# Queries stacked in 4 KB rows, early scores, panels prepared first, and unread dense products in the attention of a hybrid encoder

## The chip, the cores and the metric

The kernel runs on one core of a Trainium2 chip. The metric is device time in microseconds, as the median of the timed runs. Matrix products run on TensorE (PE in the profile), the rest on VectorE (DVE), ScalarE (ACT) and GpSimd (POOL); SyncE (SP) and ScalarE issue transfers.

## The reference

Two layers over 512 tokens of width 1024: a gated DeltaNet mixer, then sliding-window attention, each followed by an MLP and a gated per-layer embedding. The change is in the attention of the second layer:

```python
proj = h @ w_in + b_in                        # 16 query heads, 4 key/value heads of 64
q = apply_rope(proj[..., :qd] ...)            # pairs (i, i + 32) of a head are rotated
k = apply_rope(proj[..., qd:qd + kd] ...)
scores = einsum("bnqhgd,bnkhd->bnhgqk", q, kb) * 64 ** -0.5   # chunks of 64, this and the one before
m = maximum(max(scores), sink)
probs = exp(scores - m) / (sum(exp(scores - m)) + exp(sink - m))
o = einsum("bnhgqk,bnkhd->bnqhgd", probs, vb)
mix = o @ w_out + b_out
```

All is float32. The kernel splits operands of the large products in a rounded upper part (fp32r) and a remainder, and adds three products.

## The kernel before, in words

Each engine has its program, and all order between them is by semaphores. `product` (L146) issues the three matmuls of one split product. A weight matrix comes as panels of 2048 columns of 128 rows, numbered through the kernel. For each panel SP loads `wRaw`, ScalarE rounds it (`prep_hi`, L124, copy at L132) and VectorE makes the remainder (`prep_lo`, L135, L140), all in two slots; a slot's load waits for the remainder of the panel two before.

The attention has six panels, `N_SW` to `N_SW + 5`: the keys, four query panels (head j of each of the four groups; every panel has a first and a second rotary half, f = 0 and 1), and the values. `att_pe` (L1739) makes for each of the first five panels two tiles of 128 x 512 in banks 0 and 1, of 8 x 3 matmuls each, and waits for `qk_t` before it writes a bank again. `att_dve` (L1894) first makes the remainder of the next panel, then scales both tiles out of the banks (L1909), applies the rotation (L1915 to L1921) to `rot`, and takes the lower parts (L1926) once ScalarE has rounded the upper ones (`qkHi`, L1847). The parts live in the memory of `aH` and `aL`; the keys and each query panel have two rows of 512.

The scores need the rows in another order, head dimensions on 64 partitions and positions along the row. `stack` (L1702) moves them by transfers from one place of the on-chip memory to another: for each half and part, 4 transfers of 64 KB with pieces of 256 bytes for queries, 8 of 32 KB for keys. SP moves the upper parts, between its loads (`att_sp`, L1718), ScalarE the lower ones, in between its copies (`att_act`, L1834). TensorE makes the value panel, then waits for all of them and for `v_ok`.

Then come 16 blocks (`ATB`), i = 4 t + g: 128 positions, one key/value head with its four query heads. `scores(i)` writes 12 matmuls into bank i mod 4, VectorE takes maxima (`maxima`), ScalarE exponentials (`exps`, L1860), VectorE the probabilities (L1970, L1972), TensorE transposes them (L1828), ScalarE or VectorE copies them (`keep` L1872, L1982), and `values` (L1812 to L1815) multiplies them with the values; `out_hi` and `out_lo` split the result. TensorE is two blocks ahead with its scores and one behind with its values. In block 4 (`i == KVH`) ScalarE and VectorE also prepare the first panel of the output projection (L1890, L1986). After block 15 comes `out_pe`, then the second MLP.

## Time and profile before

| | us |
|---|---|
| timed runs | 1500.47, 1511.27, 1516.33 (median 1511.27) |
| profiled execution, its own time | 1499.67 |
| its span | 1497.70 |
| TensorE busy | 1455.9 (97%) |
| VectorE busy | 801.1 (53%) |
| ScalarE busy | 541.9 (36%) |
| mean granted clock of TensorE | 0.979 |

Durations and places in the span are those of the profiled execution; its time is 1.97 us over its span. A matmul's busy time in the profile includes its modelled end, so the starts of two successive ones tell the pace. In the timeline a number in brackets is the idle time before an instruction, with what ended it.

### The profile page before, as it was taken

How to read it: one execution, taken by the hardware profiler on the slowest of the kernel's cores; microseconds unless marked ns; L12 is line 12 of the kernel's file. 1: busy time of each engine (PE TensorE's matmuls, PEld its weight loads, DVE VectorE, ACT ScalarE, POOL GpSimd, SP SyncE). 2: the span in 40 equal slices, each digit the busy share in tenths (PEclk: the TensorE clock that was granted, in tenths of full speed). 3: DMA queues.
4: the chain of work that ended last, by engine and by line, in shares of the span. 5: the costliest groups of instructions: out<-in, count | busy, mean ns of one | idle time of the engine just before them, and what ended most of it. 6: DMA issues, size and time to landing. Idle time of an engine off the chain costs nothing.

```text
span 1497.7 us, 19380 instructions
## 1 busy us (share of the span) xinstructions
PE 1455.9 (97%) x7270; PEld 1202.1 (80%) x7270; DVE 801.1 (53%) x1132; ACT 541.9 (36%) x820; POOL 268.0 (18%) x269
## 2 busy tenths in 40 slices
PE   7899999999989999999999999999999999999998
PEld 5788888888877888888888777866888888888877
DVE  5555666666647434334356587556443443434655
ACT  7334343434225314232243442244341322314344
POOL 5644444535203100000002120000200000000211
PEclk9999999999999999999999999769999999999998
DMA  6212121110112232323222328511323223232221
GB/s 174 60 29 57 29 57 40 44 49 21 43 56 92 92 112 85 112 84 103 94 85 86 111 57 169 113 29 43 113 85 112 85 92 105 84 112 85 85 85 56
DMA packets 163810, 120.73 MB, mean 81 GB/s; under 512 B 44417, under 2 KB 161442, under 8 KB 163746
## 3 DMA queue, kind: packets, MB, share of 16 engines
q1 hardware_dynamic: 152210, 116.71, 26.1%
q10 hardware_dynamic: 11536, 3.15, 1.0%
q8 instruction: 42, 0.69, 0.2%
q14 instruction: 22, 0.18, 0.0%
HBM read 112.50 MB, written 2.10 MB: 77 GB/s over the span
## 4 chain that ended last, share of the span: by engine, by line
PE 79%; DVE 10%; ACT 4%; issue 3%; DVEq 1%; DMA 1%; ACTq 1%; SPq 1%; POOL 0%; POOLq 0%
PE psum L148 22%; PE psum L150 22%; PE psum L149 21%; PE psum L830 3%; PE psum L821 3%; DVE wL L140 2%; ACT wH L132 1%; PE psum L837 1%; DVE bL L1274 1%; ACT taps L676 1%; DVE hT L1475 1%; PE psum L1828 1%; DVE acc L1473 1%; PE psum L784 1%; PE psum L785 0%
## 5 line engine op out<-in xcount | busy, mean ns | idle before, releaser
L148 PE MATMUL psum<-aH,wH 128*128 128x512 f32 x896 | 363.0, 405 | 5.2 <-DVE wL L140 3.2
L150 PE MATMUL psum<-aL,wH 128*128 128x512 f32 x896 | 350.6, 391 | 0.0
L149 PE MATMUL psum<-aH,wL 128*128 128x512 f32 x896 | 349.9, 391 | 0.0
L140 DVE TENSOR_TENSOR wL<-wRaw,wH 128x2048 fp32r<-128x2048 f32 (+2 forms) x126 | 250.7, 1993 | 135.5 <-ACT wH L132 129.9
L148 PE MATMUL psum<-bH,wH 128*128 128x512 f32 x720 | 285.0, 396 | 5.7 <-DVE pleT L1909 3.2
L150 PE MATMUL psum<-bL,wH 128*128 128x512 f32 x720 | 280.8, 390 | 0.0
L149 PE MATMUL psum<-bH,wL 128*128 128x512 f32 x720 | 280.6, 390 | 0.0
L132 ACT CAST wH<-wRaw 128x2048 fp32r<-128x2048 f32 (+2 forms) x110 | 199.2, 1815 | 192.0 <-PE psum L150 191.8
L148 PEld LDWEIGHTS psum<-aH,wH 128*128 128x128 f32 x896 | 169.2, 189 | 37.1 <-DVE wL L140 3.4
L150 PEld LDWEIGHTS psum<-aL,wH 128*128 128x128 f32 x896 | 168.6, 188 | 36.3
L149 PEld LDWEIGHTS psum<-aH,wL 128*128 128x128 f32 x896 | 169.2, 189 | 30.6 <-issue 0.5
L148 PEld LDWEIGHTS psum<-bH,wH 128*128 128x128 f32 x720 | 135.5, 188 | 35.2 <-DVE wL L140 4.3
L150 PEld LDWEIGHTS psum<-bL,wH 128*128 128x128 f32 x720 | 135.3, 188 | 28.6
L149 PEld LDWEIGHTS psum<-bH,wL 128*128 128x128 f32 x720 | 135.5, 188 | 27.2 <-issue 0.5
L1460 DVE TENSOR_TENSOR hid<-hid 128x512 f32<-128x512 f32 x64 | 44.3, 692 | 149.4 <-ACT hid L1443 149.4
L1284 POOL COPY sqSum<-sqT 128x512 f32<-128x512 f32 x6 | 3.9, 649 | 656.4 <-ACT sqT L1267 641.9
L1470 DVE TENSOR_TENSOR acc<-psum,acc 128x512 f32<-128x512 f32 x64 | 44.2, 690 | 137.3 <-PE psum L150 137.3
L1443 ACT ACTIVATE hid<-psum 128x512 f32<-128x512 f32 x64 | 38.4, 600 | 208.1 <-PE psum L150 208.0
L929 ACT COPY xScaled<-psum 128x512 f32<-128x512 f32 x56 | 33.0, 589 | 154.3 <-PE psum L837 126.5
L1287 POOL TENSOR_TENSOR sqSum<-sqSum,sqT 128x512 f32<-128x512 f32 x40 | 55.7, 1392 | 135.5 <-ACT sqT L1267 114.7
L676 ACT ACTIVATE taps<-psum,colsB 128x512 f32<-128x512 f32 (+1 forms) x96 | 58.1, 690 | 15.2 <-DVE work L703 11.3
L830 PEld LDWEIGHTS psum<-xScaled 128*128 128x128 f32 x384 | 46.5, 191 | 21.2 <-ACT xScaled L929 13.9
(291 smaller groups left out, 1730.8 us busy)
## 6 DMA issues: line engine op xcount, KB each, us to landing
wRaw<-in_mlp_w_up SPq DMA_DIRECT2D x64, 512.0 KB
wRaw<-in_mlp_w_down SPq DMA_DIRECT2D x64, 512.0 KB
wRaw<-in_dn_w_in SPq DMA_DIRECT2D x32, 512.0 KB
wRaw<-in_ple_w_gate SPq DMA_DIRECT2D x16, 512.0 KB
wRaw<-in_sw_w_in SPq DMA_DIRECT2D x16, 256.0 KB
wRaw<-in_sw_w_out SPq DMA_DIRECT2D x16, 256.0 KB
wRaw<-in_dn_w_out SPq DMA_DIRECT2D x8, 384.0 KB
work<-in_x SPq DMA_DIRECT2D x4, 512.0 KB, 4.9
```

What stands on the lines that cost most here:

```text
L132: last = [nc.scalar.copy(o, r) for o, r in zip(panel_parts(wH, slot, n, True), panel_parts(wRaw, slot, n, False))][-1]
L140: last = [nc.vector.tensor_tensor(o, r, h_.bitcast(F32), ALU.subtract) for o, r, h_ in zip(*([v if half is None else v[:, half * v.shape[1 ...
L148: nc.tensor.matmul(o, wh, xh, start=first, stop=False)
L149: nc.tensor.matmul(o, wl, xh, start=False, stop=False)
L150: return nc.tensor.matmul(o, wh, xl, start=False, stop=last)
L676: last = nc.scalar.activation(taps[:, c, c:S], bank[b % 2][:, 0:S - c], ACT.Copy, scale=convW[:, CONV - 1 - c, bass.ds(b * HEADS_A + h, 1)])
L821: per_tile(lambda t: nc.tensor.matmul(bank[BY][:, rng(t)], lowT[:, t, :], inv[:, t, :], start=True, stop=True)).then_inc(t_done, 1)
L830: per_tile(lambda t: nc.tensor.matmul(bank[BX][:, rng(t)], invT[:, t, :], tMask[:, t, :], start=True, stop=True)).then_inc(p_done, 1)
L1287: nc.gpsimd.tensor_tensor(sqSum[:], sqSum[:], sqT[:, m % 2, :], ALU.add).then_inc(sq_used, 1)
L1443: nc.scalar.activation(hid[:, m % 2, :], bank[m % 2], ACT.Relu).then_inc(hid_f, 1)
L1460: nc.vector.tensor_tensor(hid2[:, m % 2, :], hid[:, m % 2, :], hid[:, m % 2, :], ALU.mult)
L1470: nc.vector.tensor_tensor(acc[:, m, :], bank[4 + m % 2], acc[:, m, :], ALU.add).then_inc(down_read, 1)
```

## The change

The upper and lower parts of two successive query panels are now written interleaved by chunk, one row of 1024 for each half (`placed`, `by_chunk`), so one transfer moves 32 partitions of 4 KB into `qS`, 8 for two panels and one part. The keys are written sorted by even and odd chunk and move in 8 transfers of 64 KB instead of 16. `stack(queue, w, i)` moves the keys (w = 0), query panels 1 and 2 (w = 1), and 3 and 4 (w = 2). SP issues the keys' upper part after it has loaded panel `N_SW + 4`, and the query stacks after its last load; ScalarE issues the lower ones in iterations 2, 4 and at the end.

On ScalarE the rounding of a panel comes ahead of the rotated rows of the panel before; on VectorE the remainder of panel j + 2 comes right behind the evacuation of panel j, ahead of its rotation.

TensorE makes, once the keys and the first query stack are there, the first head pair's half of the scores of blocks 0 to 3; it waits for the values ahead of the third. Then it issues `keep_clock(10)`: ten 128x128 by 128x512 matmuls into bank 7, whose results nothing reads. It waits for the second stack, makes the other half of blocks 0 and 1, and issues 8 more; blocks 0 to 3 have 5 more each ahead of their wait for the probabilities, and blocks 0 and 1 of the loop make the other half of the scores of blocks 2 and 3.

```diff
--- before.py
+++ after.py
@@ -1647,7 +1647,19 @@
 
         mlp_mem.close()
 
-        qkHi, qkLo = [[a[:, 2 * i:2 * i + 2, :] for i in range(4)] for a in (aH, aL)]
+        def stack_parts(a):
+            rows = [a[:, 2 * i:2 * i + 2, :].rearrange("p a b -> p (a b)") for i in range(4)]
+            return [[rows[0][:, f * S:(f + 1) * S] for f in range(2)], rows[1:3], [rows[3], rows[0]]]
+        qkHi, qkLo = stack_parts(aH), stack_parts(aL)
+
+        def placed(parts, j, f):
+
+            if j == 0:
+                return parts[0][f].rearrange("p (o m c) -> p m o c", o=2, c=CH)
+            return parts[1 + (j - 1) // 2][f].rearrange("p (n r c) -> p n r c", r=2, c=CH)[:, :, (j - 1) % 2]
+
+        def by_chunk(rows, j):
+            return rows.rearrange("p (m o c) -> p m o c", o=2, c=CH) if j == 0 else rows.rearrange("p (n c) -> p n c", c=CH)
 
         qS = sb("qS", [P, 2, 2, 2, S // CH, 2, CH], F32R)
         kS = sb("kS", [P, 4 * S + 2 * P], F32R)
@@ -1663,10 +1675,9 @@
         qk_r = sem("qk_r")
         qk_hi = sem("qk_hi")
         qk_lo = sem("qk_lo")
-        hi_moved = [sem("hi_moved0"), sem("hi_moved1")]
-        lo_moved = [sem("lo_moved0"), sem("lo_moved1")]
-        k_hi_moved = [sem("k_hi_moved0"), sem("k_hi_moved1")]
-        k_lo_moved = [sem("k_lo_moved0"), sem("k_lo_moved1")]
+        hi_moved = [sem("k_hi_moved"), sem("qa_hi_moved"), sem("qb_hi_moved")]
+        lo_moved = [sem("k_lo_moved"), sem("qa_lo_moved"), sem("qb_lo_moved")]
+        MOVED = 16 * 2 * KVH
         v_ok = sem("v_ok")
         sc_done = sem("sc_done")
         sc_read = sem("sc_read")
@@ -1699,21 +1710,19 @@
                 for r in range(2):
                     sp.dma_start(dst[r * HD:(r + 1) * HD, a], src[a, r]).then_inc(panel_in[n % 2], PANEL_INC // 4)
 
-        def stack(queue, j, f, i):
-
-            ready, part, moved = ((qk_hi, qkHi, hi_moved if j else k_hi_moved), (qk_lo, qkLo, lo_moved if j else k_lo_moved))[i]
-            queue.wait_ge(ready, 2 * j + f + 1)
-            for g in range(KVH):
-                src = part[j % 4][g * HALF:(g + 1) * HALF, f, :].bitcast(F32)
-                r = (g // 2) * HD + f * HALF
-                if j:
-                    dst = qS[r:r + HALF, (j - 1) // 2, g % 2, i, :, (j - 1) % 2, :]
-                    queue.dma_start(dst.bitcast(F32), src.rearrange("p (n c) -> p n c", c=CH)).then_inc(moved[f], 16)
-                    continue
-                c0 = (2 * (g % 2) + i) * S
-                for odd in range(2):
-                    dst = kS[r:r + HALF, c0 + odd * S // 2:c0 + (odd + 1) * S // 2].rearrange("p (m c) -> p m c", c=CH)
-                    queue.dma_start(dst.bitcast(F32), src.rearrange("p (m o c) -> p m o c", o=2, c=CH)[:, :, odd]).then_inc(moved[f], 16)
+        def stack(queue, w, i):
+
+            ready, part, moved = ((qk_hi, qkHi, hi_moved), (qk_lo, qkLo, lo_moved))[i]
+            for f in range(2):
+                queue.wait_ge(ready, 4 * w + f + 1)
+                for g in range(KVH):
+                    src = part[w][f][g * HALF:(g + 1) * HALF].bitcast(F32)
+                    r = (g // 2) * HD + f * HALF
+                    if w:
+                        dst = qS[r:r + HALF, w - 1, g % 2, i].rearrange("p n r c -> p (n r c)")
+                    else:
+                        dst = kS[r:r + HALF, (2 * (g % 2) + i) * S:(2 * (g % 2) + i + 1) * S]
+                    queue.dma_start(dst.bitcast(F32), src).then_inc(moved[w], 16)
 
         def att_sp(sp):
 
@@ -1724,14 +1733,10 @@
                     load_rotary(sp, j - 1)
                 else:
                     load_square(sp, N_SW + j, square_panel(sw_w_in[0], 0, D + (256 if j else 0)))
-                if j in (2, 3):
-                    stack(sp, 0, j - 2, 0)
-                elif j >= 4:
-                    for f in range(2):
-                        stack(sp, j - 3, f, 0)
-            for j in range(3, GRP + 1):
-                for f in range(2):
-                    stack(sp, j, f, 0)
+                if j == GRP:
+                    stack(sp, 0, 0)
+            stack(sp, 1, 0)
+            stack(sp, 2, 0)
             for j in range(4):
                 sp.wait_ge(panel_lo, N_SWOUT + j - 1)
                 load_mixer_out(sp, j)
@@ -1776,14 +1781,7 @@
                 if t % 2:
                     last.then_inc(tile_done, 1)
 
-            for f in range(2):
-                pe.wait_ge(k_hi_moved[f], 16 * KVH * 2)
-                pe.wait_ge(k_lo_moved[f], 16 * KVH * 2)
-                pe.wait_ge(hi_moved[f], 16 * KVH * GRP)
-                pe.wait_ge(lo_moved[f], 16 * KVH * GRP)
-            pe.wait_ge(v_ok, NT)
-
-            def scores(i):
+            def scores(i, heads=range(2)):
                 t, g = i // KVH, i % KVH
                 if i >= 4:
                     pe.wait_ge(sc_read, i - 3)
@@ -1791,13 +1789,19 @@
                 for c in range(2):
                     apart = S // 2 if c else S // 2 - CH
                     nk = 2 if c or t else 1
-                    for jp in range(2):
+                    for jp in heads:
                         o = bank[i % 4][:, (2 * c + jp) * P:(2 * c + jp) * P + nk * CH].rearrange("p (a k) -> p a k", a=nk)
                         q = [qS[rows, jp, g % 2, part, 2 * t + c].rearrange("p r c -> p (r c)") for part in range(2)]
                         k = [kS[rows, (2 * (g % 2) + part) * S + t * CH:(2 * (g % 2) + part) * S + t * CH + 2 * apart]
                              .rearrange("p (a k) -> p a k", a=2)[:, 0:nk, 0:CH] for part in range(2)]
                         last = product(o, q[0], q[1], k[0], k[1], True, True)
-                last.then_inc(sc_done, 1)
+                if 1 in heads:
+                    last.then_inc(sc_done, 1)
+
+            def keep_clock(count):
+
+                for _ in range(count):
+                    nc.tensor.matmul(bank[7], wH[:, n % 2, 0:P], X[0][:, 0, :], start=True, stop=True)
 
             def values(i):
 
@@ -1814,12 +1818,26 @@
                     nc.tensor.matmul(o[:, 0:2 * P], vT[0:CH, 0, d], probsT[i % 2][0:CH, 0:2 * P], start=True, stop=True)
                 nc.tensor.matmul(o[:, 2 * P:4 * P], vT[:, t, d], probsT[i % 2][:, 2 * P:4 * P], start=True, stop=True).then_inc(pv_done, 1)
 
-            scores(0)
-            scores(1)
+            for w in range(2):
+                pe.wait_ge(hi_moved[w], MOVED)
+                pe.wait_ge(lo_moved[w], MOVED)
+            pe.wait_ge(qk_t, 2 * GRP + 2)
+            for i in range(4):
+                if i == 2:
+                    pe.wait_ge(v_ok, NT)
+                scores(i, [0])
+            keep_clock(10)
+            pe.wait_ge(hi_moved[2], MOVED)
+            pe.wait_ge(lo_moved[2], MOVED)
+            scores(0, [1])
+            scores(1, [1])
+            keep_clock(8)
             for i in range(ATB):
                 t = i // KVH
                 if i + 2 < ATB:
-                    scores(i + 2)
+                    scores(i + 2, [1] if i < 2 else range(2))
+                if i < KVH:
+                    keep_clock(5)
                 pe.wait_ge(pr_ok, i + 1)
                 if i >= 2:
                     pe.wait_ge(pt_ok[i % 2], i // 2)
@@ -1833,20 +1851,23 @@
 
         def att_act(act, u, O):
             n0 = N_SW
+
+            def upper(j):
+                for f in range(2):
+                    act.wait_ge(qk_r, 2 * j + f + 1)
+                    if j == 3 and f:
+                        act.wait_ge(hi_moved[0], MOVED)
+                    nc.scalar.copy(placed(qkHi, j, f), by_chunk(rot[2 * f], j)).then_inc(qk_hi, 1)
             for j in range(GRP + 1):
                 prep_hi(act, n0 + j + 1, (n0 + j + 1) % 2)
                 if j == 0:
                     norm_act(act, u - 1)
+                if j in (2, 4):
+                    stack(act, j // 2 - 1, 1)
                 if j:
-                    for f in range(2):
-                        stack(act, j - 1, f, 1)
-                for f in range(2):
-                    act.wait_ge(qk_r, 2 * j + f + 1)
-                    if j >= 4:
-                        act.wait_ge(k_hi_moved[f], 16 * KVH * 2)
-                    nc.scalar.copy(qkHi[j % 4][:, f, :], rot[2 * f]).then_inc(qk_hi, 1)
-            for f in range(2):
-                stack(act, GRP, f, 1)
+                    upper(j - 1)
+            upper(GRP)
+            stack(act, 2, 1)
             a_ = nc.scalar
 
             def exps(i):
@@ -1895,18 +1916,18 @@
             v = nc.vector
             n0 = N_SW
             tt, st = v.tensor_tensor, v.scalar_tensor_tensor
+            prep_lo(dve, n0 + 1, (n0 + 1) % 2)
+            norm_dve(dve, u - 1)
+            dve.wait_ge(n_ok, norms_bc(u - 1))
+            dve.wait_ge(rope_ok, 1)
             for j in range(GRP + 1):
-                prep_lo(dve, n0 + j + 1, (n0 + j + 1) % 2)
-                if j == 0:
-                    norm_dve(dve, u - 1)
                 dve.drain()
-                if j == 0:
-                    dve.wait_ge(n_ok, norms_bc(u - 1))
-                    dve.wait_ge(rope_ok, 1)
                 r0 = R_BQ + 2 * (j - 1) if j else R_BK
                 for f, tf in enumerate((t1, t2)):
                     dve.wait_ge(tile_done, tiles_before(n0 + j) + f + 1)
                     tt(tf, bank[f], rBC[:], ALU.mult).then_inc(qk_t, 1)
+                if j < GRP:
+                    prep_lo(dve, n0 + j + 2, (n0 + j + 2) % 2)
                 dve.drain()
                 b1, b2 = colsB[:, r0:r0 + 1], colsB[:, r0 + 1:r0 + 2]
                 if j:
@@ -1921,9 +1942,9 @@
                 tt(rot[2], rot[2], rot[3], ALU.add).then_inc(qk_r, 1)
                 for f in range(2):
                     dve.wait_ge(qk_hi, 2 * j + f + 1)
-                    if j >= 4:
-                        dve.wait_ge(k_lo_moved[f], 16 * KVH * 2)
-                    tt(qkLo[j % 4][:, f, :], rot[2 * f], qkHi[j % 4][:, f, :].bitcast(F32), ALU.subtract).then_inc(qk_lo, 1)
+                    if j == 3 and f:
+                        dve.wait_ge(lo_moved[0], MOVED)
+                    tt(placed(qkLo, j, f), by_chunk(rot[2 * f], j), placed(qkHi, j, f).bitcast(F32), ALU.subtract).then_inc(qk_lo, 1)
             for a in range(2):
                 rows = slice(a * CH, (a + 1) * CH)
                 for c in range(2):
```

## Rows read from the trace of the kernel before

**Rows 1.** Page, part 2: granted clock in 40 slices, tenths of full speed.
```profile
PEclk9999999999999999999999999769999999999998
```

**Rows 2.** Windows: us, busy us per engine (x instructions), granted clock, DMA share, GB/s.
```profile
942.00:953.90 11.90, 11.90 (x98) 11.65 (x96) 7.33 (x16) 1.22 (x2) 0.79 (x2) 1.00 0.51 106
953.90:957.00 3.10, 0.05 (x2) 0.05 (x1) 0.88 (x2) 0.00 (x0) 1.59 (x4) 0.99 0.96 214
957.00:1001.40 44.40, 42.83 (x160) 31.14 (x160) 22.31 (x76) 18.43 (x88) 0.00 (x0) 0.50 0.27 59
1001.40:1030.90 29.50, 25.86 (x161) 18.29 (x160) 21.24 (x62) 16.43 (x75) 0.00 (x0) 1.00 0.00 1
```

**Rows 3.** PE timeline, attention: start, us, line, names, [idle before <-releaser].
```profile
956.98 0.39 PE L148 MATMUL psum<-kS,qS 64*128 64x64 f32 x1 [3.05 <-DMA qS<-aL]
...
964.62 1.06 PE L1828 MATMUL psum<-ident,acc 128*64 128x128 f32 x4 [0.52 <-DVE acc L1970]
...
985.85 1.11 PE L1828 MATMUL psum<-ident,acc 128*128 128x128 f32 x4
...
992.85 1.12 PE L1828 MATMUL psum<-ident,acc 128*128 128x128 f32 x4 [1.05 <-DVE acc L1972]
...
998.55 1.11 PE L1828 MATMUL psum<-ident,acc 128*128 128x128 f32 x4
...
1001.59 0.27 PE L149 MATMUL psum<-kS,qS 64*128 64x128 f32 x1
1001.70 0.27 PE L150 MATMUL psum<-kS,qS 64*128 64x128 f32 x1
...
1002.91 0.66 PE L1828 MATMUL psum<-ident,acc 128*128 128x128 f32 x4
...
1009.67 0.66 PE L1828 MATMUL psum<-ident,acc 128*128 128x128 f32 x4
```

**Rows 4.** PE timeline, end of panel 2 and start of panel 3.
```profile
916.52 0.39 PE L148 MATMUL psum<-bH,wH 128*128 128x512 f32 x1
916.75 0.39 PE L149 MATMUL psum<-bH,wL 128*128 128x512 f32 x1
...
920.38 0.47 PE L148 MATMUL psum<-bH,wH 128*128 128x512 f32 x1 [1.66 <-DVE pleT L1909]
```

**Rows 5.** Groups of DVE by form, 896 to 954: busy, mean ns, idle before.
```profile
L140 DVE TENSOR_TENSOR wL<-wRaw,wH 128x1024 fp32r<-128x1024 f32 x6 | 7.1, 1222 | 3.9 <-ACT wH L132 3.9
L1909 DVE TENSOR_TENSOR pleT<-psum,rBC 128x512 f32<-128x512 f32 x10 | 6.7, 690 | 4.2 <-PE psum L150 2.0 <-ACT rBC L1317 1.8
...
L1915 DVE SCALAR_TENSOR_TENSOR pleT<-pleT,colsB,ropeC 128x512 f32<-128x512 f32 x5 | 3.8, 752 | 0.5
```

**Rows 6.** Tile qS, 946 to 958: issue ns min/median/max, first and last start; landing.
```profile
L1711 ACTq DMA_DIRECT2D qS<-aL x8: 592/638/822, 948.2 to 953.0; - x8
...
DMA to landing us min/median/max: 2.1/2.1/3.7
```

**Rows 7.** DMA view, 949 to 953 (stacking) and 4.5 to 7.5 (loads of x).
```profile
DMA packets 3029, 0.73 MB, mean 182 GB/s; under 512 B 3029, under 2 KB 3029, under 8 KB 3029
...
DMA packets 349, 1.25 MB, mean 418 GB/s; under 512 B 43, under 2 KB 43, under 8 KB 349
```

**Rows 8.** ACT timeline, block 4's preparation.
```profile
987.48 1.90 ACT L132 CAST wH<-wRaw 128x2048 fp32r<-128x2048 f32 x1
```

**Rows 9.** DVE timeline, block 4's preparation.
```profile
989.42 2.29 DVE L140 TENSOR_TENSOR wL<-wRaw,wH 128x2048 fp32r<-128x2048 f32 x1 [2.21 <-ACT wH L132]
```

**Rows 10.** PE timeline, another wait, in the DeltaNet loop.
```profile
441.77 0.80 PE L784 MATMUL psum<-vNew,trig 128*128 128x128 f32 x2 [2.94 <-DVE vNew L986]
```

**Rows 11.** Windows behind that wait, columns as in rows 2.
```profile
441.60:445.00 3.40, 3.23 (x12) 2.94 (x13) 0.70 (x3) 0.00 (x0) 0.00 (x0) 0.51 0.71 216
445.00:448.00 3.00, 3.00 (x19) 2.42 (x19) 1.25 (x4) 0.37 (x1) 0.00 (x0) 1.00 0.31 104
```

## The prediction

> **What bounds the kernel.** The page's slices first: TensorE is busy nearly everywhere, and in two slices of forty its granted clock falls to 0.7 and 0.6 of full speed [rows 1]. The windows by stage put that in one place. Up to 953.9 TensorE works at full clock on the dense projection of the values; it then idles about 3 us, and from 957.0 to 1001.4 the attention's blocks run at clock 0.50, the lower level (1.2 GHz). From 1001.4 to 1030.9 the same kind of block runs at 1.00 (2.4 GHz) [rows 2]. The timeline of PE gives the price: between the transposes of blocks 5 and 6 lie 5.70 us at half clock, between those of blocks 7 and 9 6.76 us at full clock, so 3.38 us a block [rows 3]. A full-size block at half clock costs **2.32 us** more. The change works on this stretch and on the projections ahead of it; after 1030.9 TensorE has the next dense product ready and everything shifts as one, so what the attention ends earlier, the kernel ends earlier.
>
> Basis: the profiled execution took 1499.67 us for a span of 1497.70. The three timed runs are 1500.47, 1511.27 (the median, 11.6 above the profiled one) and 1516.33.
>
> **Projections, panels first.** Before, TensorE waits 1.66 us at 920.38 in front of the third query panel [rows 4]. The chain behind it: SP issues eight key transfers ahead of the panel's load, ScalarE rounds it late, and VectorE's remainder comes last. After, no transfer stands between SP's loads up to the panel at `N_SW + 4`, and both preparing engines take the next panel ahead of the rotation. VectorE's work per panel is 2 evacuations (0.69 each), a remainder of 2 x 1.22 (started 0.1 us apart, so 2.35), 4 rotations (0.75 each in the row, started some 0.67 apart), 2 sums and 2 lower parts of 0.69 [rows 5]: some 9.2 us. TensorE's 48 products at 0.227 us [rows 4] take 10.9 us. By my count of the order, the first evacuation of the next panel ends 10.7 to 11.4 us after the last tile of the one before, just when TensorE needs the bank: a wait of up to 0.3 us remains. **Gain 1.6 us**; bounds 0 (the wait turns into one for the bank) and 1.66. The key transfers lie beside products. On SP the next load queued behind them waits for a remainder that comes later anyway, and ScalarE's eight issues of about 0.64 us [rows 6] end before the rotated rows it next waits for. The value projection thus ends at 952.3 instead of 953.9.
>
> **Stacking.** Transfers that must follow the last query panel grow from 16 of 64 KB to 16 of 128 KB, since panels 3 and 4 share a row: 2.1 MB. SP can issue from about 945.7, ScalarE from 946.4, eight each at about 0.63 us, and the median landing is 2.1, the longest 3.7 [rows 6]. At the rate of loads in 4 KB rows, 418 GB/s [rows 7], the issues bound it and the last lands at 953.9. At the rate of today's stacking, 182 GB/s [rows 7], the bytes take 11.5 us and it lands near 958.5. I take 957.5, nearer the slow end, because that row is this transfer between the same memories. A first load of the output projection now queues behind these on SP; its panel is not prepared before block 4, so that costs nothing.
>
> **Opening of the attention.** From 952.3: 24 early products (four half scores) at 0.112 us, the pace at full clock [rows 3], 2.7 us; a wait for the values' evacuation is covered by the first two halves; 10 dense products, 2.3 us; TensorE asks for the last stack at 957.3. So it waits 0 to 1.2 us where it waited 3.05 [rows 3], with dense products right before. I take it that the clock stays. The first complete score is then ready at about 958.1 instead of 959.6. Then 0.7 + 8 x 0.227 + 0.7 + 5 x 0.227 gives block 0's transposes at 962.4, about when the softmax chain delivers; before, 964.62.
>
> **Blocks 0 to 4.** At full clock TensorE's own work is 0.6 (transposes), 1.0 (values), 1.36 (scores): 2.96 us. Five dense products add 1.14 in blocks 0 to 3; there they partly exceed the wait they fill (4.1 against the 3.38 of the other engines), 0.7 us a block. Transposes come at 965.0, 969.1, 973.2 and, for block 4, 976.5; before, block 4's were at 985.85 [rows 3]. So the gain stands at **9.35 us** here.
>
> **The hole before block 5.** The change leaves the preparation of the first output panel in block 4: ScalarE's rounding (1.90 us, right behind block 4's transposes) and VectorE's remainder (2.29) stand ahead of block 5's probabilities [rows 8, 9]. That chain made 7.00 us from transposes 4 to 5 [rows 3], of which TensorE at half clock filled all but 1.05. At full clock the transposes are 0.45 shorter, so it is 6.6 us, and TensorE has 2.96 us of work: it **waits 3.6 us**, with no dense product there. Two waits of this trace show what follows: 3.05 us ahead of 957.0, and 2.94 us ahead of 441.77, both ending at half clock [rows 2, 3, 10, 11]. So I expect the clock to fall here. Block 5's transposes come at 983.2 (before: 992.85).
>
> **From block 5 on.** If nothing fell, block 7 would be at 983.2 + 6.76 = 990.0 against 1002.91, and the rest is as before: 12.9 us less, **1486.7**. Each block at half clock adds 2.32. Before, the clock came back 8.5 us after block 5's transposes [rows 2, 3], 1.5 blocks. The timed runs are 0.8, 11.6 and 16.7 us longer, which I read as the clock coming back 0.3, 5.0 and 7.2 blocks later; never coming back in the attention would be 8.5 blocks or 19.7 us, just above the longest run. Laid on the new kernel, 1.5, 1.8, 6.5 and 8.7 blocks give 1490.2, 1490.9, 1501.8 and 1506.9. Their mean is **1497**, the forecast: 14 us under the median shown, 2.5 under the profiled execution. This case's own range is 1488 to 1510.
>
> **A rule against this.** In the rows the clock stayed at 0.50 for 44 us although TensorE was busy for over nine tenths of them [rows 2]. The Trainium skill, "TensorE: Matmul & The Clock Gate", Part 1, says that sustained activity releases the throttle; busy time in this trace does not bear that out. By it the loss after the hole would be about one block, and the kernel about 1489.
>
> **The rivals.**
> A, the forecast: kept up to block 4, lost in the hole, back at a varying block. 0.63.
> B, the clock survives the hole: 1486.7. Against it, shorter waits already ended at half clock. 0.07.
> B2, it falls but returns with the first blocks (where the rule above would be right): 1486.7 + 2.3 = 1489. For it, after the fall ahead of 441.77 the clock was back by 445 [rows 10, 11]; there half of the products were dense ones, and blocks of the attention needed far longer. 0.10.
> C, **slower**: the last stack lands late. From a wait of about 2.9 us (landing at 960.2), or if early scores and wait together are too thin, the clock falls before block 0. Score and dense products then take about twice their 0.112 and 0.227 us, so block 0 comes at 960.2 + 2.6 + 3.6 + 1.3 + 2.3 = 970.0, 5.4 late, with 13 dense products in it; the 15 dense products of blocks 1 to 3 add up to 6.8, less what block 1's wait hides, and block 4 comes some 10.5 us later than before. Coming back as in the profile gives 1510, never coming back 1499.7 + 19.7 + 10.5 = 1530. For it: the bytes behind the last panel double; against it, even the slow rate lands at 958.5. 0.09, of which 0.05 slower by over 1%.
> D, the spread of the runs is not the clock's: then the gain over the profiled execution for the clock back after as many blocks, 1499.7 - 1490.2 = 9.5 us, comes off the median: 1502. 0.11.
> That the dense products are not executed as written, or the clock is not their doing, lies inside A and C.
>
> **Numbers.** Over 1% means under 1496.2 or over 1526.4, about what a measurement of this kernel tells from no change. A puts some 0.28 below 1496, the rest within; B and B2 add 0.17: faster 0.45. Slower 0.05 from C. Same 0.50, the rest of A and C and all of D. The range takes A's own, B's time at the lower end and C's with the clock back as in the profile at the upper: 1486 to 1511.
>
> **What would show it.** Right: no wait of TensorE at the third query panel; value projection ending near 952.3; clock 1.00 through blocks 0 to 4, their transposes near 962, 965, 969, 973, 976.5; a wait of about 3.6 us before block 5 and clock 0.50 after it. Wrong: the clock at 0.50 before block 0 (C), no fall at the hole (B), a landing far from 957.5, or a stretch from block 0 to block 4 far from 14 us. The forecast fails most easily by how long the clock stays low after block 5: one block is 2.3 us, and nothing in the rows fixes the number.

## The result: 0.6% faster

The changed kernel's median is 1494.96 us (15 runs, 1489.72 to 1509.72), that of the kernel before 1502.71 (15 runs, 1497.04 to 1517.09): a ratio of **0.9941**, 95% interval 0.9912 to 0.9970. Here and below the ratio is an estimate over the runs of both kernels made beside each other, not the quotient of the two medians, and it leaves out runs more than 1.5% above the fastest of their kernel (one of experiment 8, and one of the kernel before beside it). The three runs of before shown with the profile lay high; their median of 1511.27 was not typical. The profiled execution took 1496.54 us for a span of 1494.6, against 1499.67 and 1497.7. Everything after the start stands 0.8 us later in this execution than in the profiled one of before (block 1's first matmul waits at 897.53 instead of 896.68), and the output projection's first product starts at 1027.73 instead of 1030.92. So the stretch between is 4.0 us shorter.

The page's slices of the granted clock (the answer to [rows 1]) have one low slice less:

```profile
PEclk9999999999999999999999999979999999999998
```

The windows of the changed kernel answer to [rows 2]; the columns are the same:

```profile
957.90:961.30 3.40, 2.55 (x17) 2.03 (x16) 1.11 (x6) 0.05 (x1) 0.00 (x0) 0.98 1.12 222
961.30:964.70 3.40, 3.40 (x12) 2.37 (x10) 1.82 (x9) 2.82 (x18) 0.00 (x0) 0.51 1.13 228
964.70:985.20 20.50, 19.44 (x113) 13.85 (x112) 12.24 (x43) 11.34 (x51) 0.00 (x0) 1.00 0.05 9
985.20:1002.30 17.10, 14.90 (x51) 10.22 (x52) 10.36 (x29) 6.46 (x33) 0.00 (x0) 0.50 0.28 62
1002.30:1027.80 25.50, 22.40 (x140) 15.69 (x139) 18.14 (x54) 13.93 (x62) 0.00 (x0) 1.00 0.00 1
```

Before, the clock was at 0.50 for 44.4 us in one piece. Now it falls twice: near 961.2, for 3.4 us, and near 985.1, for 17.1 us. Between them 20.5 us of the attention run at full clock, which none of blocks 0 to 5 did before.

The timeline of TensorE in the attention, for [rows 3]. L148 is a score product (the first of the early ones, then the first after the last stack), L1804 the unread dense products, L1846 the transposes of blocks 0, 4, 5, 6 and 8:

```profile
953.18 0.29 PE L148 MATMUL psum<-kS,qS 64*128 64x64 f32 x1
...
955.70 2.58 PE L1804 MATMUL psum<-bH,wH 128*128 128x512 f32 x10
959.14 0.26 PE L148 MATMUL psum<-kS,qS 64*128 64x64 f32 x1 [0.85 <-DMA qS<-aL]
...
960.59 3.29 PE L1804 MATMUL psum<-bH,wH 128*128 128x512 f32 x8
...
966.25 0.60 PE L1846 MATMUL psum<-ident,acc 128*64 128x128 f32 x4
...
980.85 0.66 PE L1846 MATMUL psum<-ident,acc 128*128 128x128 f32 x4
...
987.40 1.12 PE L1846 MATMUL psum<-ident,acc 128*128 128x128 f32 x4 [3.26 <-DVE acc L1993]
...
993.10 1.11 PE L1846 MATMUL psum<-ident,acc 128*128 128x128 f32 x4
...
1003.40 0.66 PE L1846 MATMUL psum<-ident,acc 128*128 128x128 f32 x4
```

TensorE now waits 0.85 us for the last stack instead of 3.05. Eight dense products from 960.59 take 3.29 us where ten from 955.70 took 2.58: the fall of 961.2 lies in them. Block 4's transposes come at 980.85 (before: 985.85). Then comes a wait of **3.26 us** ahead of block 5, from 984.14 to 987.40; the clock falls some 0.9 us after its start. Blocks 5 and 6 lie 5.70 us apart, as before at half clock.

In front of the third query panel [rows 4] TensorE has no wait left (no bracket in its row):

```profile
919.69 0.47 PE L148 MATMUL psum<-bH,wH 128*128 128x512 f32 x1
```

The last stack, the answer to [rows 6] and to the first row of [rows 7] (issues from ScalarE, landing times of all, then the packets of 947 to 953):

```profile
L1725 ACTq DMA_DIRECT2D qS<-aL x8: 514/680/1168, 947.5 to 953.2; - x8
...
DMA to landing us min/median/max: 2.3/4.3/5.8
```

```profile
DMA packets 474, 1.34 MB, mean 223 GB/s; under 512 B 148, under 2 KB 148, under 8 KB 474
```

A transfer in 4 KB rows takes 4.3 us in the median to land and 5.8 at most. In the first 0.9 us of these 6 nothing moved. Over 949 to 953, the 4 us of the first row of [rows 7], the rate was:

```profile
DMA packets 397, 1.09 MB, mean 271 GB/s; under 512 B 132, under 2 KB 132, under 8 KB 397
```

So the bytes doubled, and the rate rose by half, from 182 to 271 GB/s; it stayed far from 418.

The preparation still stands between blocks 4 and 5, on ScalarE and on VectorE, and takes as long as before [rows 8, 9]:

```profile
982.03 1.90 ACT L132 CAST wH<-wRaw 128x2048 fp32r<-128x2048 f32 x1
```

```profile
983.96 2.29 DVE L140 TENSOR_TENSOR wL<-wRaw,wH 128x2048 fp32r<-128x2048 f32 x1 [1.76 <-ACT wH L132]
```

### The profile page after: what moved, and what is told of

Same layout as the page of the kernel before. It is cut to its first block, busy times and chain, and to the rows that moved or that the text cites. A ratio compares the mean times of both kernels' runs of the same rounds, so it can differ in the third digit from the quotient of the medians.

```text
span 1494.6 us, 19405 instructions
## 1 busy us (share of the span) xinstructions
PE 1455.1 (97%) x7308; PEld 1201.6 (80%) x7308; DVE 800.5 (54%) x1132; ACT 541.5 (36%) x820; POOL 267.7 (18%) x269
## 4 chain that ended last, share of the span: by engine, by line
PE 81%; DVE 9%; ACT 4%; issue 3%; DVEq 1%; DMA 1%; ACTq 1%; POOL 0%; SPq 0%; POOLq 0%
PE psum L148 22%; PE psum L150 22%; PE psum L149 22%; PE psum L830 3%; PE psum L821 3%; DVE wL L140 2%; ACT wH L132 1%; PE psum L837 1%; DVE bL L1274 1%; ACT taps L676 1%; DVE hT L1475 1%; PE psum L1846 1%; PE psum L1804 1%; DVE acc L1473 1%; PE psum L784 1%
## 5 line engine op out<-in xcount | busy, mean ns | idle before, releaser
L148 PE MATMUL psum<-aH,wH 128*128 128x512 f32 x896 | 363.2, 405 | 5.2 <-DVE wL L140 3.2
L148 PE MATMUL psum<-bH,wH 128*128 128x512 f32 x720 | 285.1, 396 | 4.2 <-DVE wL L140 1.8
L148 PEld LDWEIGHTS psum<-aH,wH 128*128 128x128 f32 x896 | 169.2, 189 | 37.1 <-DVE wL L140 3.4
L148 PEld LDWEIGHTS psum<-bH,wH 128*128 128x128 f32 x720 | 135.5, 188 | 33.9 <-issue 3.8
```

What stands on the lines that cost most here:

```text
L148: nc.tensor.matmul(o, wh, xh, start=first, stop=False)
```

## The experiments

**The theory**: the change's gain is the time that the attention runs at full clock; the dense products hold it up to block 4, the wait ahead of block 5 loses it, and the number of blocks until it returns makes the spread between runs. **Rival 1**: the reordering and the stacking bring the gain, the products only cost. **Rival 2** (D of the prediction): spread and level have nothing to do with the clock. **Rival 3**: a fall needs one wait of about 3 us.

Diffs are against the changed kernel, except where the text says otherwise. Each experiment has its own runs of the kernel before beside it, with a median of 1502.32 us for 1 to 4, 1500.60 for 5 to 8 and 1502.56 for 9 and 10; "profiled" means one execution.

**1. No products.**

```diff
-            keep_clock(10)
...
-            keep_clock(8)
...
-                if i < KVH:
-                    keep_clock(5)
```

> The changed kernel without any of its 38 unread dense products; everything else as changed. Theory (the clock): TensorE waits some 3 us or more for the last stack, the clock falls before block 0 and stays at 0.50 through most blocks, so the time is that of the kernel before less what reordering gives at half clock (1.6 us of the projections, and about 1 of the early scores): 1498 to 1503 us, with the same spread of some 20 us between runs as before. Rival (the reordering brings the gain, and the products only cost 0.7 us a block): 1492 to 1493 us, 2 to 3 us below the changed kernel.

Measured: median 1500.54 us (1497.59 to 1519.20, 12 runs), ratio to the kernel before 0.9994 [0.9950, 1.0037]. Its windows, and the first score product after the last stack in its timeline:

```profile
960.00:963.00 3.00, 1.06 (x11) 0.92 (x9) 0.00 (x0) 0.00 (x0) 0.79 (x2) 0.94 1.05 233
963.00:1000.00 37.00, 32.60 (x119) 22.46 (x119) 20.18 (x69) 16.63 (x80) 0.00 (x0) 0.50 0.32 67
```

```profile
964.12 0.39 PE L148 MATMUL psum<-kS,qS 64*128 64x64 f32 x1 [3.06 <-DMA qS<-aL]
```

The wait is as long as before, 3.1 us (961.06 to 964.12); the clock falls in it, near 962.6, and stays at 0.50 to 1000. Reordering and stacking alone are worth nothing that 12 runs can tell. The spread of 22 us is that of before. Rival 1, which asked for 1492 to 1493, falls.

**2. Products alone**, in the kernel before:

```diff
+            keep_clock(13)
             for f in range(2):
                 pe.wait_ge(k_hi_moved[f], 16 * KVH * 2)
...
+                if i < KVH:
+                    keep_clock(5)
                 pe.wait_ge(pr_ok, i + 1)
```

> The kernel before with dense products alone: 13 ahead of its wait for the stacks, 5 in each of blocks 0 to 3; no reordering, stacking as before. Theory: the clock is kept up to block 4 and falls in the wait ahead of block 5, as in the changed kernel; without the 1.6 us of the projections and the early scores it lies 1 to 3 us above the changed kernel: 1496 to 1498. Rival (reordering and stacking are needed for the gain): 1503 or more, no faster than before.

Measured: median 1497.88 us (1492.28 to 1512.10, 12 runs), ratio 0.9984 [0.9946, 1.0021]. The runs form two groups, seven up to 1498.01 and five from 1505.41 to 1512.10. Windows of the profiled one:

```profile
955.00:985.80 30.80, 29.99 (x192) 23.26 (x191) 15.61 (x59) 13.68 (x66) 1.82 (x5) 1.00 0.44 93
985.80:1003.00 17.20, 14.38 (x49) 9.71 (x49) 10.46 (x29) 7.09 (x36) 0.00 (x0) 0.52 0.27 62
```

The mechanism is as expected: full clock up to the wait ahead of block 5 (985.36 to 988.62), then the fall in it, near 986.6. The median is as expected too, but the interval takes in no change, so that products alone gain something is not shown by the times, only by the windows.

**3. The wait ahead of block 5 filled.** The products go to a score bank that has been read (`keep_clock` takes the bank as a second argument):

```diff
+                if i == KVH + 1:
+                    pe.wait_ge(sc_read, i)
+                    keep_clock(14, bank[(i + 3) % 4])
                 pe.wait_ge(pr_ok, i + 1)
```

> The changed kernel with 14 more unread dense products (3.2 us at full clock) in TensorE's wait ahead of block 5, into a score bank that has been read. Theory: the clock no longer falls there, blocks 5 to 15 run at 3.38 us each, the profiled span shows clock 1.00 from about 965 to the end of the attention; block 7's transposes come near 990 plus the 1 to 2 us lost at the opening: median 1487 to 1490, and the spread between runs shrinks to a few us. Rival D (the spread and the level of the runs are not the clock's): median 1494 to 1496 and the spread stays some 15 to 20 us. Rival (the wait is not what makes it fall): the clock falls later all the same, 1493 to 1496.

Measured: median 1491.36 us (1486.92 to 1493.50, 10 runs), ratio 0.9915 [0.9883, 0.9946].

```profile
964.00:980.00 16.00, 16.00 (x93) 11.55 (x92) 10.50 (x40) 8.62 (x48) 0.00 (x0) 1.00 0.17 35
980.00:986.60 6.60, 6.60 (x36) 4.80 (x35) 4.34 (x9) 4.37 (x12) 0.00 (x0) 1.00 0.01 2
986.60:1000.00 13.40, 12.40 (x81) 9.14 (x80) 10.51 (x33) 8.11 (x40) 0.00 (x0) 1.00 0.35 78
1000.00:1026.00 26.00, 22.90 (x130) 16.19 (x130) 18.77 (x48) 14.12 (x54) 0.00 (x0) 1.00 0.00 1
```

No fall in the attention, the opening included: TensorE there waited 0.42 us for the last stack in this execution. TensorE is busy through 980.0 to 986.6. The 0.54 us waits of the later blocks and one of 2.02 us stay, and the clock stays up. The spread is 6.6 us instead of 20, as the theory has it and neither of its rivals. The median is 1.4 over the range's upper end: five of its ten runs have a mean clock of only 0.990 to 0.991, which a fall at the opening would explain; no trace shows it.

**4. The preparation moved instead.**

```diff
-                if i == KVH:
+                if i == 1:
                     prep_hi(act, N_SWOUT, N_SWOUT % 2)
...
-                if i == KVH:
-                    prep_lo(dve, N_SWOUT, N_SWOUT % 2)
+                if i in (2, 3):
+                    prep_lo(dve, N_SWOUT, N_SWOUT % 2, i - 2)
```

> The changed kernel with the preparation of the first output panel moved: ScalarE rounds it in its iteration 1, VectorE makes the remainder in two halves (1.2 us each) in blocks 2 and 3, where TensorE has its dense products. No product added. Theory: the wait of 3.3 us ahead of block 5 goes, at most 1 us appears in blocks 2 to 4, the clock stays: time as with the wait filled or up to 3 us below, since the chain of 6.6 us shrinks to 3.4: 1484 to 1488. Rival (wait moved, not removed): TensorE waits 2 us or more in block 2 or 3, the clock falls there, 1494 or more.

Measured: median 1496.40 us (1494.19 to 1509.91, 12 runs), ratio 0.9963 [0.9931, 0.9996]. A miss for the theory as it stood. Transposes of blocks 4 and 5, and windows:

```profile
982.89 0.65 PE L1846 MATMUL psum<-ident,acc 128*128 128x128 f32 x4 [1.03 <-DVE acc L1993]
...
987.34 1.11 PE L1846 MATMUL psum<-ident,acc 128*128 128x128 f32 x4
```

```profile
981.50:984.90 3.40, 2.37 (x14) 1.29 (x12) 2.87 (x11) 1.27 (x5) 0.00 (x0) 0.97 0.45 124
984.90:988.30 3.40, 3.40 (x16) 3.03 (x15) 1.13 (x3) 1.38 (x8) 0.00 (x0) 0.50 0.93 189
988.30:1002.00 13.70, 13.70 (x48) 9.28 (x47) 7.35 (x24) 5.75 (x29) 0.00 (x0) 0.51 0.00 0
```

The wait ahead of block 5 is gone; a wait of 1.03 us stands ahead of block 4, the first block without dense products, and the clock falls near 984.7 all the same, 1.8 us after that wait, to stay down for over 17 us. So rival 3, which was the prediction's own picture of the fall, is wrong: there was no wait of 3 us here, and one of 2.02 us late in the attention brought no fall in the same execution. That the wait of 1.03 us was the cause is not shown: the stretch without dense products begins at the same place. The clock also fell at the opening of this execution, from 960.8 to 967.6.

**5. Both waits filled**: experiment 3's edit, and

```diff
-            keep_clock(10)
+            keep_clock(14)
```

> The changed kernel with the wait ahead of block 5 filled by 14 products and 14 instead of 10 products ahead of the last stack. Theory: the short fall at the opening (3.4 us at half clock in the changed kernel's profile, some 1.5 us of time) goes too: median 1488 to 1490.5, with no run under 0.991 in mean clock. Rival (the opening's fall is set by the early scores and not by the wait of 0.9 us, or four products only delay the second half scores): the same as with the wait alone filled, 1491 to 1492.

Measured: median 1488.85 us (1488.20 to 1491.20, 6 runs), ratio 0.9933 [0.9917, 0.9949]. As expected: no run has a mean clock under 0.992; TensorE has no wait for the stack left and the clock does not fall:

```profile
956.00:964.00 8.00, 8.00 (x43) 6.36 (x42) 3.29 (x16) 2.87 (x18) 0.00 (x0) 1.00 1.12 227
964.00:985.50 21.50, 21.50 (x122) 15.41 (x120) 13.86 (x45) 12.04 (x53) 0.00 (x0) 1.00 0.05 11
985.50:1025.00 39.50, 35.40 (x210) 25.45 (x210) 29.41 (x80) 22.19 (x93) 0.00 (x0) 1.00 0.12 28
```

**6. The preparation moved, with products in blocks 4 and 5**: experiment 4's edit, `keep_clock(14)` at the opening, and

```diff
+                elif i < KVH + 2:
+                    pe.wait_ge(sc_read, i)
+                    keep_clock(5, bank[(i + 3) % 4])
```

> The preparation of the output panel moved into blocks 1 to 3, with 14 instead of 10 dense products ahead of the last stack's wait and 5 more in blocks 4 and 5. In the run with the preparation moved alone a wait of 1.03 us ahead of block 4 was enough for the clock to fall. Theory: with products there the clock stays at 1.00 from the value projection to the end of the attention; no chain of 6.6 us between blocks 4 and 5: median 1486 to 1489, 2 to 5 us under the kernel with the wait filled. Rival (the clock falls in other blocks once the products end): 1492 to 1496.

Measured: median 1489.47 us (1488.03 to 1494.31, 6 runs), ratio 0.9942 [0.9920, 0.9963]. The fall of experiment 4 is gone with products in its place. The median is 0.5 over what was expected: the shorter chain gives no time, since the moved halves and ten more products lie on the path of blocks 2 to 5 (block 7's transposes at 991.89, in experiment 5 at 992.21).

**7. Without the ten ahead of the stack.**

```diff
-            keep_clock(10)
```

> The changed kernel without the ten dense products ahead of the last stack's wait; the 8 and the 5 a block stay. Theory: TensorE waits 3.1 us there, as in the run without any products, so the clock falls before block 0; the 8 and 5 dense products run at half clock, cost 0.2 us each more, and bring the clock back within blocks 0 to 2: 1 to 4 us over the changed kernel, 1496 to 1499. Rival C of the prediction (fallen there it stays, and the products cost double): 1505 or more.

Measured: median 1497.52 us (1494.52 to 1515.43, 12 runs), ratio 0.9993 [0.9960, 1.0025].

```profile
957.70:964.50 6.80, 6.11 (x20) 5.11 (x20) 3.02 (x14) 2.88 (x18) 0.00 (x0) 0.52 1.14 232
964.50:988.40 23.90, 20.64 (x121) 14.82 (x120) 14.77 (x47) 12.07 (x53) 0.00 (x0) 0.99 0.01 3
988.40:1002.10 13.70, 13.70 (x48) 9.19 (x47) 7.48 (x25) 5.77 (x29) 0.00 (x0) 0.51 0.33 74
```

The wait is 3.04 us and the clock falls in it, near 957.4, but with the eight products (from 961.11) it is back by 964.2, ahead of block 0. Experiment 1, without any product, stayed down for 37 us from there. The rival of the prediction in which it stays down does not happen in the profiled execution; two of twelve runs, over 1510, may be such.

**8. Without products in the blocks.**

```diff
-                if i < KVH:
-                    keep_clock(5)
```

> The changed kernel with its 10 and 8 products in the opening, and none in blocks 0 to 3. Theory: blocks 0 to 3 have narrow scores and waits of about 0.4 us each at full clock, so the clock falls in one of them in most runs, and comes back as late as in the kernel before: 1498 to 1501. Rival (the opening's products are enough, and those in the blocks only cost 0.7 us each): 1492 to 1493.

Measured: median 1497.33 us (1493.25 to 1517.28, 12 runs), ratio 0.9970 [0.9948, 0.9993]. Slightly below the range expected.

```profile
962.90:966.30 3.40, 3.40 (x13) 2.39 (x11) 1.53 (x8) 2.54 (x17) 0.00 (x0) 0.63 1.15 233
966.30:969.80 3.50, 2.59 (x17) 1.90 (x16) 2.81 (x14) 2.12 (x11) 0.00 (x0) 0.86 0.18 34
969.80:997.00 27.20, 26.15 (x92) 17.01 (x92) 14.43 (x43) 11.71 (x51) 0.00 (x0) 0.52 0.14 32
```

The clock falls in the opening, returns, and falls again at about 969, ahead of block 1 (behind a wait of 0.91 us), for 27 us. So without the products in the blocks the clock is lost again, and with them it was held from block 1 up to block 4's transposes in every profiled execution.

**9. Fewer on the path**: both waits filled, 6 and 3 in place of 8 and 5.

```diff
-            keep_clock(8)
+            keep_clock(6)
...
-                    keep_clock(5)
+                    keep_clock(3)
```

> As the kernel with both waits filled (14 products ahead of the last stack, 14 ahead of block 5), with 6 instead of 8 products after the second half scores and 3 instead of 5 in each of blocks 0 to 3. There TensorE had no wait, so each product lies on the path. Theory: 10 products less are 2.3 us, less what the softmax chain then makes TensorE wait (blocks at 3.6 us instead of 4.4): median 1486.5 to 1488 if the clock holds. Rival (3 a block are too few): the clock falls in one of blocks 1 to 3 in most runs, 1491 or more, with a spread as in the run without products in the blocks.

Measured: median 1488.76 us (1485.38 to 1492.68, 6 runs), ratio 0.9913 [0.9892, 0.9934]. Its profiled execution has block 4's transposes at 977.20, 1.8 us ahead of experiment 5's, but the median is the same within its uncertainty.

**10. Half of the filling**: experiment 3 with 7 products.

> The changed kernel with 7 instead of 14 products in the wait ahead of block 5: a wait of 1.7 us remains there. Theory (the clock answers to how much of the stretch is dense, not to whether there is a wait over 3 us): since 1.03 us ahead of block 4 were enough in the run with the preparation moved, but waits of 2.0 us late in the attention are not, the result is mixed: part of the runs at 1487 to 1493, part at 1494 or more, median 1490 to 1494. Rival 1 (only a wait of about 3 us makes it fall, as the prediction had it): as with 14, 1491 or below with a spread under 7 us. Rival 2 (any gap): as the changed kernel, 1495.

Measured: median 1490.02 us (1485.24 to 1497.92, 6 runs), ratio 0.9929 [0.9902, 0.9956]. In the profiled execution a wait of 1.45 us is left ahead of block 5, and the clock holds:

```profile
983.58 0.66 PE L1849 MATMUL psum<-ident,acc 128*128 128x128 f32 x4 [1.45 <-DVE acc L1996]
```

```profile
983.50:1000.00 16.50, 15.41 (x100) 11.44 (x100) 13.11 (x42) 10.09 (x49) 0.00 (x0) 1.00 0.27 64
```

Two of the six runs, 1494.09 and 1497.92, have a mean clock of 0.990 and 0.987 as the changed kernel has. Mixed, as the theory had it, on few runs.

**The opening, over the profiled executions.** Ten kernels make the same early scores and then ask for the last stack; the times at which the clock fell and returned are read from windows of 0.5 us:

| | dense products ahead | wait, us | clock |
|---|---|---|---|
| wait before block 5 filled (3) | 10 | 0.42 | kept |
| half of the filling (10) | 10 | 0.47 | kept |
| without those in the blocks (8) | 10 | 0.66 | half for 3.4 us, from 962.0 |
| preparation moved (4) | 10 | 0.70 | half for 6.8 us, from 960.8 |
| the change | 10 | 0.85 | half for 3.4 us, from 961.2 |
| without the ten (7) | 0 | 3.04 | half for 6.8 us, from 957.4 |
| no products (1) | 0 | 3.06 | half for 37 us, from 962.6 |
| 14 ahead (5, 6, 9) | 14 | none | kept |

The same ten products thus kept the clock in two executions and lost it in three. The three had the longer waits, but by 0.2 to 0.4 us, and that the length of the wait decides is not shown by five executions.

**The spread.** Each run has a mean clock and a span, so the time it spent at half clock, over the whole kernel, is 2 x (1 - clock) x span, if there are only the two levels. Over the 15 runs of the changed kernel the time rises by 0.36 us for each us of it, with a correlation over 0.99; over 33 runs of the kernel before by 0.39, correlation 0.96. Rival 2 falls. The price per block read from the trace, 2.32 in 5.70 us, is 0.41.

| | median, us | range | before beside it | ratio to it |
|---|---|---|---|---|
| no products | 1500.54 | 1497.59 to 1519.20 | 1502.32 | 0.9994 |
| without the ten | 1497.52 | 1494.52 to 1515.43 | 1500.60 | 0.9993 |
| products alone | 1497.88 | 1492.28 to 1512.10 | 1502.32 | 0.9984 |
| without those in the blocks | 1497.33 | 1493.25 to 1517.28 | 1500.60 | 0.9970 |
| preparation moved | 1496.40 | 1494.19 to 1509.91 | 1502.32 | 0.9963 |
| preparation moved, products in 4 and 5 | 1489.47 | 1488.03 to 1494.31 | 1500.60 | 0.9942 |
| **the change** | 1494.96 | 1489.72 to 1509.72 | 1502.71 | 0.9941 |
| both waits filled | 1488.85 | 1488.20 to 1491.20 | 1500.60 | 0.9933 |
| half of the filling | 1490.02 | 1485.24 to 1497.92 | 1502.56 | 0.9929 |
| wait before block 5 filled | 1491.36 | 1486.92 to 1493.50 | 1502.32 | 0.9915 |
| both filled, fewer on the path | 1488.76 | 1485.38 to 1492.68 | 1502.56 | 0.9913 |

The intervals of the filled kernels overlap that of the change; that they are better rests on medians, on the narrower ranges and on spans of profiled executions (1484.3 to 1488.2 against 1494.6).

## Why the prediction was right, point by point

- **Projections.** Right. No wait at the third panel, and the value projection ends at 953.1, or 952.3 with the later start of 0.8 us taken off.
- **Stacking.** The landing was put 1.5 us too early, 957.5 against 959.0, of which the later start is 0.8; with that taken off it is 958.2, close to the slow bound of 958.5. ScalarE's eight issues began at 947.5 and the last only at 953.2, and that one took 5.8 us to land, not 2.1 to 3.7. From 953 to 959.5 SP's queue, where the first loads of the output projection stand behind the stack, moved 1.02 of 1.52 MB. The prediction put that load at nothing because its panel is not needed early; whether it holds up the last transfer no run tests. The Trainium skill, "DMA: Bandwidth & Descriptors", "Why small descriptors are slow (HBM only)", says that transfers within the on-chip memory don't pay for small pieces. This trace does not bear that out: pieces of 256 bytes went at 182 GB/s, rows of 4 KB at 271. It does not isolate it either, since the transfers were twice as large too. The gain in rate was used up: sharing a row between two panels doubled the bytes behind the last panel.
- **Opening.** The failed step: "I take it that the clock stays". It fell for 3.4 us behind a wait of 0.85 us, early scores and half scores. Landing and fall put block 0 at 966.25 instead of 962.4 (0.8 of it the start). Experiment 5 fills this wait, keeps the clock and has block 0 at 964.37. The clock was also kept in two executions with the change's own ten products (experiments 3 and 10), so this step holds in some executions and fails in others.
- **Blocks 0 to 4.** Right in mechanism: full clock, 14.6 us from block 0 to block 4 against 14.1 predicted. The gain at block 4 was 5.0 us instead of 9.35: 0.8 of the difference is the later start, 0.5 the blocks, the rest the opening. Experiment 8 shows that without the five a block the clock is lost in block 1, experiment 1 that without any products nothing is held.
- **The hole.** Right in place and size: 3.26 us for 3.6, clock at 0.50 from 985.2. Experiment 3 shows that filling the wait takes the fall away, and what that is worth. Wrong in its reason: a wait of about 3 us is not needed, since the fall came 0.9 us into this one, and in experiment 4 the clock fell behind a wait of 1.03 us.
- **After block 5.** The clock came back 14.9 us after block 5's transposes, 2.6 blocks; over its 15 runs the whole kernel spent 37 us at half clock in the mean, the kernel before 75 over 33 runs. The reading of the spread as returning blocks is borne out by the mean clocks.
- **The level of before.** The forecast's size against its base, 14 us, was double the 7.75 measured, because the base of three runs was high by 8.6 us. The sum from the profiled execution, 2.5 us, was nearer.
- **The number.** That 1497 came within 2.0 us of the median is luck in part, since two terms missed in opposite directions. Without any block at half clock the prediction had 1486.7; the profiled execution's 1496.54 less 2.6 blocks of 2.32 us is 1490.5, an estimate. For the blocks at half clock it took 4.6 in the mean; the median over that 1490.5 is 1.9 of them.
- **The rivals.** B (the clock survives the hole) did not come. B2 (it returns with the first blocks) did not come either: 2.6 blocks ran at half clock. At the opening, with dense products behind the fall, the clock was back in 3.4 us, and in 6.8 us in experiment 7. The Trainium skill, "TensorE: Matmul & The Clock Gate", Part 1, says that activity releases the throttle; the opening agrees with it. Behind the hole the trace does not: TensorE was busy without a wait from 987.4 to 1002.3, 14.9 us, and stayed at half clock. C's price was wrong: in experiment 7 the clock fell before block 0, and with dense products behind it block 4's transposes came at 981.26, 2.3 us after those of experiment 5 and not some 10. D is excluded by the correlation.

**Open**: what exactly makes the clock fall. Every filling of these experiments does two things at once, it takes idle time away and puts dense work in its place, and no run separates them. The length of a wait alone does not order the outcomes: 1.45 us ahead of block 5 with seven products held (experiment 10), 1.03 us ahead of block 4 with none did not (experiment 4), 2.02 us late in the attention mostly did. In two profiled executions (experiments 6 and 9) it fell for 3.4 us near 1016, in the late waits of the attention, in the others it did not. Whether the stacking in long rows gives anything by itself was not tried apart from the reordering.

## What to carry to other kernels

When a stage runs at half clock although TensorE is busy, look at what stands ahead of the fall, and put unread dense products into the waits there and behind it: a filler that stopped one wait too early, and was 0.85 us short in another, brought 7.8 us by medians, where filling both brought 11.8 against the runs beside it. Products in a wait cost nothing that showed here; products where TensorE is the bound cost 0.23 us each in the trace, though ten fewer of them (experiment 9) did not change the median. And take the mean granted clock of every run before reading a spread or a median of three: here it explained nearly all of 20 us.

## What the hardware showed that was not expected

- A wait of 1.03 us among transposes, values and narrow scores was followed by half clock (experiment 4), while waits of 2.0 us near the end of the attention mostly were not. Where a wait of 3.26 us ended at half clock, the fall came 0.9 us into it (the change).
- At half clock, blocks of 5.70 us with TensorE all but fully busy kept it there for 14 to 44 us (experiment 7, the kernel before); with eight products of 128 x 512 in the stretch full clock was back 3.4 to 6.8 us after the fall (the change, experiment 7).
- Transfers of 128 KB in 4 KB rows within the on-chip memory ran at 271 GB/s, against 182 for transfers of 64 KB in rows of 256 bytes over the same 4 us of the kernel before.
